# A two-block transformer forward pass on one core: a bias table written in 16 copies instead of 128 and read back by GpSimd, the first products reordered, and three smaller moves

## Time and profile before

| | |
|---|---|
| time, median of 3 runs | 1021.18 us (1020.94 to 1021.76) |
| the profiled execution's own time | 1021.69 us |
| its span, first to last instruction | 1019.8 us |
| mean granted TensorE clock over the span | 0.995 of full speed |
| PE busy | 995.3 us, 98% |
| DVE busy | 678.6 us, 67% |
| ACT busy | 545.8 us, 54% |
| POOL busy | 37.4 us, 4% |
| moved by DMA | 177.27 MB, mean 174 GB/s |

### The profile page before, as it was taken

One profiled execution on the slowest core, in us unless ns is written; L12 is line 12 of the kernel. 1 busy time (PEld: TensorE's weight loads), 2 busy tenths in 40 slices (PEclk: granted clock), 3 DMA queues, 4 the chain that ended last, 5 costly groups with the idle time before them and its releaser, 6 DMA issues.

```text
span 1019.8 us, 15706 instructions
## 1 busy us (share of the span) xinstructions
PE 995.3 (98%) x6371; PEld 853.0 (84%) x6371; DVE 678.6 (67%) x847; ACT 545.8 (54%) x714; POOL 37.4 (4%) x58
## 2 busy tenths in 40 slices
PE   7989999999999999999999999999999999999997
PEld 6778777898888887987889888888899888888885
DVE  4657976778777877858667656556656566555554
ACT  6747565457565565643546444544455556444452
POOL 1210000000000004100000000000000000000000
PEclk9989999999999999999999999999999999999999
DMA  8573333555656554864255655555664347555541
GB/s 287 112 206 125 124 124 123 171 185 195 206 193 197 174 165 147 258 203 142 85 186 186 206 183 188 201 174 203 189 204 145 109 161 244 172 201 188 183 165 41
DMA packets 122835, 177.27 MB, mean 174 GB/s; under 512 B 3055, under 2 KB 91578, under 8 KB 122778
## 3 DMA queue, kind: packets, MB, share of 16 engines
q1 hardware_dynamic: 118860, 168.82, 49.9%
q10 hardware_dynamic: 2702, 3.59, 1.8%
q0 software_dynamic: 1216, 4.05, 1.4%
HBM read 173.82 MB, written 2.62 MB: 173 GB/s over the span
## 4 chain that ended last, share of the span: by engine, by line
PE 72%; issue 19%; DVE 4%; ACT 2%; DMA 2%; POOL 1%; POOLq 0%; ACTq 0%; DVEq 0%
PE ps L1808 19%; PE ps L1858 16%; PE ps L1829 10%; PE ps L1857 7%; PE ps L1845 5%; PE ps L1872 2%; PE ps L1880 2%; DMA raw<-in_w_uq 1%; DVE w_lo L1062 1%; PE ps L1954 1%; PE ps L2274 1%; PE ps L2098 1%; PE ps L1860 1%; PE ps L1920 1%; PE ps L2082 1%
## 5 line engine op out<-in xcount | busy, mean ns | idle before, releaser
L1062 DVE TENSOR_TENSOR w_lo<-raw,w_hi 128x2048 fp32r<-128x2048 f32 (+3 forms) x156 | 352.2, 2261 | 133.2 <-ACT w_hi L526 132.9
L1858 PE MATMUL ps<-x_both,w_hi 128*128 128x512 f32 x992 | 342.7, 396 | 0.0
L526 ACT ACTIVATE w_hi<-raw 128x2048 fp32r<-128x2048 f32 (+3 forms) x161 | 302.3, 1880 | 70.6 <-PE ps L1808 40.5
L1857 PE MATMUL ps<-x_both,w_lo 128*128 128x256 f32 x868 | 242.0, 279 | 0.0
L1858 PEld LDWEIGHTS ps<-x_both,w_hi 128*128 128x128 f32 x992 | 179.1, 188 | 34.5
L1857 PEld LDWEIGHTS ps<-x_both,w_lo 128*128 128x128 f32 x868 | 163.6, 189 | 5.6
L771 ACT ACTIVATE work<-ps 128x512 f32<-128x512 f32 x66 | 39.3, 595 | 150.3 <-PE ps L1858 134.5
L1808 PE MATMUL ps<-w_hi,x_both 128*128 128x512 f32 (+1 forms) x320 | 101.3, 387 | 0.5 <-ACT work L696 0.5
L1808 PE MATMUL ps<-w_hi,hid_hi 128*128 128x512 f32 x240 | 93.9, 391 | 0.2 <-DVE work L1374 0.2
L1808 PE MATMUL ps<-w_hi,hid_lo 128*128 128x512 f32 x240 | 93.4, 389 | 0.0
L1808 PE MATMUL ps<-w_lo,hid_hi 128*128 128x512 f32 x240 | 93.4, 389 | 0.0
(11 more groups left out here) (289 smaller groups left out, 1291.7 us busy)
## 6 DMA issues: line engine op xcount, KB each, us to landing
raw<-in_ffn_w SPq DMA_DIRECT2D x66, 1024.0 KB, 5.1
raw<-in_w_up SPq DMA_DIRECT2D x22, 1024.0 KB, 5.0
raw<-in_hgrn_w_in SPq DMA_DIRECT2D x16, 1024.0 KB, 5.3
raw<-in_w_in SPq DMA_DIRECT2D x12, 1024.0 KB, 5.2
raw<-in_moba_w_in SPq DMA_DIRECT2D x12, 1024.0 KB, 5.3
raw<-in_w_down SPq DMA_DIRECT2D x11, 1024.0 KB, 4.9
raw<-in_w_out SPq DMA_DIRECT2D x4, 1024.0 KB, 5.1
raw<-in_hgrn_w_out SPq DMA_DIRECT2D x4, 1024.0 KB, 6.3
```

What stands on the lines that cost most here:

```text
L526: act.activation(w_hi[:, n % RING, 0:kc * cols], raw[:, n % RING, 0:kc * cols], ACT.Copy).then_inc(s["hi_ready"], 1)
L1062: dve.tensor_tensor(w_lo[:, n % RING, sl], raw[:, n % RING, sl], f32(w_hi[:, n % RING, sl]), ALU.subtract).then_inc(s["lo_ready"], 1)
L1857: pe.matmul(out[:, 0, :], w_lo[:, n % RING, at], x_hi[:, k, :], start=False, stop=False)
L1858: ins = pe.matmul(out, w_hi[:, n % RING, at], x_both[:, k, :, :], start=(k == 0), stop=(k == DC - 1))
```

## The change

- `bias_scratch` holds 16 copies (`COPIES`), not 128. ACT's write to it leaves its place after line 665 and is issued in `fill_work(8)`, in unit 8 of the attention of layer one. The wait ahead of `hi(5)` is now for `taps_done`, an older copy of ACT's own.
- The reading back leaves ACT (line 975). POOL issues eight transfers of 16 partitions (128 KB each) after its load of the gains `gain(6)`, during the first granules of the second feed-forward, in front of `inverse_rms(6)`.
- `x_hi` of chunks 0 and 1 is written by DVE, ahead of its `x_lo`, not by ACT. `first_product` goes in pairs of chunks: `x_hi w_hi` for both, `x_lo w_hi` for both, then the next pair, and `x_hi w_lo` at the end. `keep_busy` ahead of the first transpose has 2 matmuls, not 4.
- ACT copies the first half of q before v.
- The fifth round of key choice, counted from the first after unit 0, moves from after unit 2 to after unit 1.
- In the recurrence `choose(5)` comes after `wider(16)`, and the 12 matmuls of granule `nh + 6` come before the wait for `x_ready` 8.

```diff
+COPIES = 16
-        bias_scratch = nc.dram_tensor("bias_scratch", (P, HEADS, BIAS_LEN), F32, kind="Internal").ap()
+        bias_scratch = nc.dram_tensor("bias_scratch", (COPIES, HEADS, BIAS_LEN), F32, kind="Internal").ap()
...
@@ gpsimd
             pool.wait_ge(s["row_ready"], step(5, 1, 1))
             gain(6, a["norm_mix_2"][1])
+            pool.wait_ge(s["bias_out"], 16)
+            for r in range(0, P, COPIES):
+                skew = bass.AP(bias_scratch.tensor, P - 1 - r, [[HEADS * BIAS_LEN - 1, COPIES], [BIAS_LEN, HEADS], [1, S]])
+                pool.dma_start(bias[r:r + COPIES], skew).then_inc(s["bias_in"], 16)
             inverse_rms(6)
@@ scalar
             first_cols = 2 * granules[0][5]
-            first_operand_hi(0, 2)
             act.wait_ge(s["first_in"], 16)
...
             act.activation(bias_row[:, :], ps[0:HEADS, 2, 0:BIAS_LEN], ACT.Copy).then_inc(s["bias_sb"], 1)
-            act.wait_ge(s["bias_sb"], 1)
-            act.dma_start(bias_scratch.rearrange("t h j -> h t j"), bias_row.unsqueeze(1).broadcast_to((HEADS, P, BIAS_LEN))).then_inc(s["bias_out"], 16)
+            act.wait_ge(s["taps_done"], 1)
             hi(5)
...
-            act.wait_ge(s["products_done"], G["uv"] + 1)
-            act.activation(v_b, ps[:, 2:4, :], ACT.Copy).then_inc(s["kv_copied"], 1)
-            for t in range(TT):
+
+            def copy_qb(t):
...
+            copy_qb(0)
+            act.wait_ge(s["products_done"], G["uv"] + 1)
+            act.activation(v_b, ps[:, 2:4, :], ACT.Copy).then_inc(s["kv_copied"], 1)
+            copy_qb(1)
...
             def fill_work(u):
+                if u == 8:
+                    act.wait_ge(s["bias_sb"], 1)
+                    act.dma_start(bias_scratch.rearrange("t h j -> h t j"), bias_row.unsqueeze(1).broadcast_to((HEADS, COPIES, BIAS_LEN))).then_inc(s["bias_out"], 16)
...
-            act.wait_ge(s["bias_out"], 16)
-            skew = bass.AP(bias_scratch.tensor, P - 1, [[HEADS * BIAS_LEN - 1, P], [BIAS_LEN, HEADS], [1, S]])
-            act.dma_start(bias, skew).then_inc(s["bias_in"], 16)
@@ vector
             def first_operand_lo(c0, c1):
                 for c in range(c0, c1):
-                    dve.wait_ge(s["xhi_ready"], 2 * (c // 2) + 2)
+                    if c < 2:
+                        dve.wait_ge(s["first_x"], c + 1)
+                    else:
+                        dve.wait_ge(s["xhi_ready"], 2 * (c // 2))
...
+            dve.wait_ge(s["vcol_done"], 1)
+            dve.wait_ge(s["xt_done"], 1)
+            for c in range(2):
+                dve.tensor_scalar(x_hi[:, c, :], ps[:, 0, 256 * c:256 * c + 256], vcol[:, 0, V_MIX1 + c:V_MIX1 + c + 1], None,
+                                  ALU.mult).then_inc(s["first_x"], 1)
             first_operand_lo(0, 4)
...
-            ROUNDS = {0: 1, 2: 1, 3: 1, 4: 1}
+            ROUNDS = {0: 1, 1: 1, 3: 1, 4: 1}
...
-                        dve.wait_ge(s["bias_in"], 16)
+                        dve.wait_ge(s["bias_in"], 16 * (P // COPIES))
...
             for level in range(8):
-                if level < 6:
+                if level < 5:
                     choose(level)
                 if level >= 1:
                     dve.wait_ge(s["pairs_done"], level + 1)
                     wider(2 ** (level - 1))
+                if level == 5:
+                    choose(level)
@@ tensor
-            keep_busy(7, 4)
+            keep_busy(7, 2)
             turn_x(0)
...
-                for low in range(2):
-                    if low:
-                        split_ready(n)
-                    for k in range(kc):
...
+                for k0 in (0, 2):
+                    if n == 0 and k0 == 0:
+                        pe.wait_ge(s["first_hi"], 1)
+                    else:
+                        pe.wait_ge(s["hi_ready"], n + 1)
+                    for x in (x_hi, x_lo):
+                        for k in (k0, k0 + 1):
+                            first_ready(chunks + k, x is x_lo)
+                            for t in range(TT):
+                                pe.matmul(ps[:, 4 + t, 0:cols], x[:, chunks + k, P * t:P * t + P], w_hi[...],
...
+                split_ready(n)
+                for k in range(kc):
+                    for t in range(TT):
+                        ins = pe.matmul(ps[:, 4 + t, 0:cols], x_hi[...], w_lo[...],
...
+            token_tile(nh + 6, 1, 0, 6, True, False)
             pe.wait_ge(s["x_ready"], 8)
             pe.wait_ge(s["og_copied"], 1)
...
             values(0)
-            token_tile(nh + 6, 1, 0, 6, True, False)
             pe.wait_ge(s["cross_copied"], 1)
             values(1)
```

More of the change, by code:

```diff
@@ L297, in build @@
         table = sb("table", [NBUCKET + 1, HEADS])
-        names = """small_in mix_in first_in first_hi first_lo gate_scale taps_in pos_in posrow_in const_in shapes_in gain_in table_in masks_in final_in final2_in bias_out bias_in out_done
+        names = """small_in mix_in first_in first_hi first_lo gate_scale first_x taps_in pos_in posrow_in const_in shapes_in gain_in table_in masks_in final_in final2_in bias_out bias_in out_done
             setup warmed vrow_T vcol_done taps_T taps_done bias_ps bias_sb trig_ready
@@ L1912, in turn_x, with first_ready @@
                         ins.then_inc(s["xt_done"], 1)
-            def first_ready(c):
-                pe.wait_ge(s["xlo_ready"], c + 1)
+            def first_ready(c, low):
+                if low:
+                    pe.wait_ge(s["xlo_ready"], c + 1)
+                else:
+                    pe.wait_ge(s["first_x"] if c < 2 else s["xhi_ready"], c + 1 if c < 2 else c - 1)
             def turn_half(k, t, half):
@@ L1941, in first_product @@
                 _, _, _, kc, _, cols = granules[n]
-                for low in range(2):
-                    if low:
-                        split_ready(n)
-                    for k in range(kc):
[L1946 to L1955, removed]
+                for k0 in (0, 2):
+                    if n == 0 and k0 == 0:
+                        pe.wait_ge(s["first_hi"], 1)
+                    else:
+                        pe.wait_ge(s["hi_ready"], n + 1)
[3 more added lines that the diff above has]
+                            for t in range(TT):
+                                pe.matmul(ps[:, 4 + t, 0:cols], x[:, chunks + k, P * t:P * t + P], w_hi[:, n % RING, cols * k:cols * k + cols],
+                                          start=(n == 0 and k == 0 and x is x_hi), stop=False)
+                split_ready(n)
+                for k in range(kc):
+                    for t in range(TT):
+                        ins = pe.matmul(ps[:, 4 + t, 0:cols], x_hi[:, chunks + k, P * t:P * t + P], w_lo[:, n % RING, cols * k:cols * k + cols],
+                                        start=False, stop=(n == 1 and k == kc - 1))
                 ins.then_inc(s["products_done"], 1)
```

## The result

The changed kernel takes 1016.18 us (median of 4 runs, 1015.47 to 1016.53); the kernel before takes 1021.06 beside it (1020.80 to 1021.76). The ratio is 0.9947, with a 95% interval of 0.9934 to 0.9959: some 5 us faster, where 10.2 were forecast, and outside the range of 1009.6 to 1014.8. The profiled execution took 1015.47 around a span of 1013.7, so 6.2 less than the profiled one of before.

The account below looks back on a forecast made before the run. PE bounds the kernel, working 995.3 of 1019.8 us, so only its gaps, clock and own instructions count. Gains of 7.8 + 0.8 + 1.6 = 10.2 from the median 1021.18 gave 1011.0 us, 8-in-10 range 1009.6 to 1014.8.

Parts of the forecast that it names:

- the chain bias write: Ahead of the index scores: the 31.5 us write delays w_uq to 14.8 us; PE idles 4.5 us, then half clock.
- Part one: Write moved out of the way: gap, half clock and q-copy wait go, granule 11 starts 7.8 us earlier.
- The gap that stays: PE's wait ahead of the index scores at line 2003: 0.1 us left instead of 4.54.
- the swap of the q copy: Ahead of granule 11, ACT copying q before v: worth 0.2 to 0.5 us, included in the 7.8.
- PE's three unit waits: Ahead of transposes in the units: their sum of 1.1 us is kept, change 0, between -0.3 and +0.5.
- Part two: The start: PE's low products begin earlier, w_lo ending the stage; gain 0.8 us, bounds 1.3 and -1.0.
- Part three: The recurrence: waits of 1.4 and 0.2 us go, gain 1.6, down to -0.3 if margins are missed.
- The margins behind `values(0)`: In the recurrence, ahead of PE's transposes: margin falls from 3 to about 1 us but holds; next ones 0.1 to 0.3.
- Part four: Reading back by POOL in the second feed-forward: 8 to 12 us, loads delayed 2 to 3 within 4.3 slack, gain 0.
- rival C: Second feed-forward: reading back crowds the weight loads, eight transfers of 14.8 us each; 23 us lost, 1034; chance 0.03.
- the milder form: Rival C's crowding of loads, eating the gain to within 2 us of before; chance 0.02.
- Rivals A and B: A: second PE gap of 1 us after 58 us, 1014.9, chance 0.13; B: w_uq stays slow, 1018.8, 0.05.

Follow-up runs that it names:

- e7_small_write: Kernel before, with 16 copies written instead of 128 at the old place, read back late by ACT in eight pieces: 1014.45 us, ratio 0.9931.
- e4_pool_spread: Changed kernel, with POOL's eight read-back pieces spread out, one for every third granule from n0 + 5 on: 1011.96 us, ratio 0.9900.
- e12_start_undone: e4_pool_spread with the old start: first x_hi on ACT, old order of products, four keep_busy matmuls: 1011.91 us, ratio 0.9906.
- e5_copies128: Changed kernel with COPIES = 128: 1.5 MB written at unit 8, one read over 128 partitions by POOL at the early place: 1017.66 us, ratio 0.9969.
- e9_pad64: e4_pool_spread with 64 further, already met semaphore waits on PE at its very start: 1009.69 us, ratio 0.9883.
- e2_act_early: Changed kernel, with the eight pieces read back by ACT's queue at the same early place, not by POOL: 1014.06 us, ratio 0.9929.
- e6_copies32: Changed kernel with COPIES = 32: four read-back pieces of 32 partitions at the same early place: 1012.85 us, ratio 0.9917.

## Why the prediction was half right

- **What bounds the kernel, and the chain bias write, `w_uq`, `hi(10)`, relus, gap, half clock:** right. e7_small_write shows it by one edit.
- **Part one, 7.8:** 7.87 (8.94 less 1.07). The gap that stays was put at 0.1 and is 0.2, and the swap of the q copy is worth 0.5 (the wait of 0.53 that e7_small_write keeps), the upper end of what was said. PE has no new wait behind the write at unit 8. PE's three unit waits went from 1.1 to 0.9, inside the bounds.
- **Part two, 0.8:** 1.07 at the first low product, and it is `w_lo` that ends the stage, as said; between 0.6 and 0.9 in the comparison of e4_pool_spread with e12_start_undone.
- **Part three, 1.6:** both waits go, 1.63. The margins behind `values(0)` held. What I had not seen is that a stall of supply can fall into the same place. The kernel before had it too, 0.18 long; it takes 1.4 back in e4_pool_spread, not in the changed kernel.
- **Part four, 0:** this step failed, and by itself it makes the forecast wrong: "I take 8 to 12 us, by the row of the same operation, in which a load is delayed by 2 to 3 us: inside the slack". Two sizes in it were off, and the first by itself makes the miss.
  - The delay. The row is of one transfer over 128 partitions; the new one is eight over 16 each. Those move 150 GB/s with all engines held and lasted 13.3 us, not 8 to 12, and the load was 6 us late (11.1 for 5), not 2 to 3. ACT got its weights 4.25 us after it wanted them. The Trainium skill's rule on how many engines a transfer is spread over (DMA: Bandwidth & Descriptors, "Why a DMA increments its semaphore by 16 and not by 1") lets the pieces of 16 partitions use all 16. The trace agrees (106.8% of the 16); but engines in use are not bytes moved.
  - The slack. I took 4.3, from the end of DVE's `lo` to PE. But in the fixed orders of ACT and DVE the next hidden chunk (L1505, `hid_hi`, `hid_lo`, L1473) stands behind this `hi` and `lo`, and PE waits for it. In the kernel before it is 8.50 us from the start of ACT's `hi` at 551.37 to PE at 559.87, now 6.88 (545.14 to 552.02): the slack is 1.6 at ACT, 1.5 by the rule from four kernels. With what the load itself has to spare ahead of ACT, that rule gives 3.4 in all, not 4.3. The delay that I expected, 2 to 3, would still have fitted: in e5_copies128 the load was 3.5 late and PE waited 0.16. And with the 4.3 that I took, a delay of 6 would still have cost 1.8.

  The second half, 1.88 of half clock, was in the price of rival C and follows from the wait. So what came true is that rival's mechanism in a still milder form than the one it named: in the same place, for one load and not for 118 us, and it took back 4.6 of 10.6 us, where the milder form was to leave at most 2. With 0.05 for C it had far too little: the write at the old place, the nearest row of a narrow transfer, moved 0.10 MB in 2 us at 43.5%, so 115 GB/s at a full share, which was a warning of what such a shape can cost.
- **Rivals A and B:** no second gap of 1 us after 59 (0.2), and `w_uq` lands in 4.1.

With part four mended, the change gives about what was forecast, 1011.0: e4_pool_spread 1011.96 with a stall of 1.4, e9_pad64 1009.69 without it.

## What to carry to other kernels

Price a transfer by a row of its own shape, partitions per transfer above all: eight narrow pieces were not an eighth of one wide transfer each, and in one bundle they held off the load behind them. Take the slack of a load not from its last use but from every step that stands behind it in its engines' written orders; the smallest of these counts. And when an edit with a clear gain in the timeline gives nothing in the time, look for idle with nothing waited for: it can belong to where the instructions lie, and some padding in an idle stretch tests that.

## What the runs showed of the hardware

- Reads of the bias table from DRAM, with the 16 engines at a share of 85 to 112%: on POOL's queue 150 GB/s in pieces of 16 partitions, 205 in pieces of 32, 300 over 128; on ACT's queue 190 and 335 in pieces of 16 and over 128. On POOL's queue the traces have this read in packets of 4 KB, on ACT's in packets of 1 KB.
- The first packet of a weight load came 4.35 us after its issue while POOL's pieces were under way, 2.7 us beside one read over 128 partitions, and 1.0 in quiet.
- PE fell to half clock behind idle times of 4.54 and 2.72 us, and not behind one of 1.53 (e2_act_early) or 0.78 (e6_copies32), with a granted clock of 1.00. But in e5_copies128 it fell at 158.4, behind one of 1.33: the length of the idle time alone doesn't decide it.
- A stall of PE of up to 1.7 us, for which no semaphore is the reason, stands behind the same number of PE's instructions in eleven kernels, and in the nine that have over 0.1 us of it PE goes on 1.4 us after a 16 KB instruction packet has ended. It was gone with 33 more instructions on PE, placed 480 us ahead of it.
